# Routed-expert block: every item's rows added into one copy of the output, in a chain, where two alternating copies took them

## The chip, the cores and the metric

The kernel runs on one core of one Trainium2 chip. The metric is the device time of one execution in microseconds (us). The kernel before was timed three times: 1404.11, 1408.82 and 1414.78 us, median 1408.82 us. One more execution was taken with the hardware profiler.

## The reference, cut to what matters

One layer of an encoder: a mixing stage (spatial gating and a Fourier part), then a mixture of 64 experts over 1024 tokens of 1024 channels, all in float32. Only the end of the mixture and the final norm bear on the change:

```
eidx, gates = route(hn, w_router, router_bias)          # 8 of 64 experts per token
routed = routed_experts(hn, eidx, gates, w_gate, w_up, w_down)
    # per block of up to 128 tokens of one expert:
    #   out = (silu(xb @ w_gate[e]) * (xb @ w_up[e])) @ w_down[e] * gate
    #   y = y.at[tok].add(out)
shared = (silu(hn @ ws_gate) * (hn @ ws_up)) @ ws_down
h = h + routed + shared
return rms_norm(h, final_norm_g)
```

## The kernel before

**Stages.** Up to about 450 us the kernel does the mixing stage, the router and the shared expert. Then comes the loop over *items*. An item is one block of up to 128 tokens that chose the same expert; in these inputs there are 93 items for 64 experts, so some experts have one item and some have two or more. Three items are one turn (`TURN = 3`), and buffers that rotate by item have three places, `u = 0, 1, 2`. After the loop comes the final norm over eight blocks of 128 rows.

**One item, engine by engine.** GpSimd (POOL) gathers the item's token rows from `hn_rows_dram` into `Xg` with an indirect DMA, four items ahead. TensorE (PE) transposes them (L464), multiplies by gate and up weights (`gate_up`, L721), transposes the result (`turn_h`, L743) and multiplies by the down weights (`down`, L735). VectorE (DVE) forms `hh` from the silu, the gate value and the up product (`gated_h`, L1290). ScalarE (ACT) copies the result out of PSUM into `ob[:, u, :]` (`evac_out`, L940). POOL then issues an indirect DMA with `compute_op=add` (`add_rows`, L1492; called *the add* below) that adds the 128 rows of `ob`, 512 KB, into rows of `y_rows_dram`. The weights of an expert (3 MB: `raw_gu` twice, `raw_dn` once) are loaded by the sync engine's queue (SP), and ACT and DVE split them into a high and a rest part.

**POOL's order.** In item `i` POOL does, in this order: `keep_gate(i+1)` (waits for the transposes of item i+1, then a small copy of the gate column, L1474), `gather(i+4)` (L1461, L1464), `add_rows(i-1)` (L1481, L1492). POOL works in order, so whatever the add waits for also holds up the next item's gate copy and gather. The gate copied by `keep_gate(i+1)` is first read by DVE's `hh` of item i+1, about one item later.

**Copies of the output.** `y_rows_dram` holds three copies of the output rows, each of `ROWS = 1152` rows. Copy 0 starts as h plus the shared expert; copies 1 and 2 are filled with zeros (L340). Items of even number add into copy 0, those of odd number into copy 1, the last three into copy 2 (`copy_row`, `late_row`). The same row may be named by two items, and an accumulating transfer reads and later writes its row, so two adds into one copy must not be in flight together. With two alternating copies, add `i` waits for the landing of add `i-2`; in the last turn, whose three adds share copy 2, adds wait for the one right ahead.

**The end.** When the adds of all but the last turn have landed and the last weights are split, SP loads copy 0 into `ya_in` (eight transfers of 512 KB, L439) and half of copy 1 into `yb_in` (L441); after the last `gate_up` it loads the other half (L446). DVE adds the two (`both_copies`, L1358, eight instructions). After the last add has landed, SP loads copy 2 into `yc_in` (L452), DVE adds that (`last_copy`, L1363), ACT squares and sums (L789), POOL makes the root (L1412, L1414), DVE scales (L1374) and SP stores (L455).

Of the kernel before, what the change touches and what calls it, by code (L numbers as in the profile page):

```python
# [23 lines left out]
P = 128  # L24
# [38 lines left out]
def build(nc, x, g1, w_in, ln_g, ln_b, wsT, bsT, ga, gb, w_out, g2, w_router, rbias, wg, wu, wd,  # L63
          sg, su, sd, dft_pos, dft_ch, gf, out, hn_d, y_d):
    ctx = ExitStack()
    with ctx:
        top = [nc.sbuf_base]

        def place(name, shape, dt, at=None):

            size = 2 if dt in (BF16, F16) else 4
            n = size
            for s in shape[1:]:
                n *= s
            n = (n + 31) // 32 * 32
            if at is None:
                at = top[0]
                top[0] += n
            return nc.alloc_sbuf_tensor_at(name, shape, dt, offset=at)
# [126 lines left out]
        ya_in = place("ya_in", [P, NC, D], F32, U_AT)  # L206
        yb_in = [place("yb_in0", [P, NC // 2, D], F32, Z_AT), place("yb_in1", [P, NC // 2, D], F32, T_AT)]
        yc_in = place("yc_in", [P, NC, D], F32, X_AT)
# [55 lines left out]
        s_yl = [sem(f"y_last_in{c}") for c in range(NC)]  # L264
        s_both, s_sum = sem("copies_summed"), sem("last_copy_summed")
        s_sqf, s_rf, s_of, s_ost = sem("sqf"), sem("rstdf"), sem("out_rows"), sem("out_stored")
# [6 lines left out]
        yv2 = y_d[ROWS:2 * ROWS, :].rearrange("(c p) d -> c p d", p=P)  # L273
        yv3 = y_d[2 * ROWS:3 * ROWS, :].rearrange("(c p) d -> c p d", p=P)
        y23_flat = y_d[ROWS:3 * ROWS, :].rearrange("(p r) (a f) -> p (r a) f", p=P, f=P)
        dump_flat = y_d[S:ROWS, :].rearrange("p (a f) -> p a f", f=P)
# [38 lines left out]
        def _(sp):  # L315
# [23 lines left out]
            sp.dma_start(dump_flat, zero[:, None, :].to_broadcast([P, KD, P])).then_inc(s_dz, 16)  # L339
            sp.dma_start(y23_flat, zero[:, None, :].to_broadcast([P, 2 * (ROWS // P) * KD, P])).then_inc(s_zst, 16)  # L340

# [96 lines left out]
            for c in range(NC):  # L438
                sp.dma_start(ya_in[:, c, :], yv[c]).then_inc(s_x[c], 16)  # L439
                if c < NC // 2:  # L440
                    sp.dma_start(yb_in[0][:, c, :], yv2[c]).then_inc(s_x[c], 16)  # L441
            last = last_item(sp)
            sp.wait_ge(s_gu, last + 1)
            sp.sem_inc(s_turn_sp, 1)
            for c in range(NC // 2, NC):
                sp.dma_start(yb_in[1][:, c - NC // 2, :], yv2[c]).then_inc(s_x[c], 16)  # L446
            n = turns(sp)
# [3 lines left out]
            for c in range(NC):  # L451
                sp.dma_start(yc_in[:, c, :], yv3[c]).then_inc(s_yl[c], 16)  # L452
            for c in range(NC):
# [548 lines left out]
        def _(dv):  # L1002
# [270 lines left out]
            for c in range(2, NC):  # L1273
                slot_marks(c)
                if c == 5:
                    shared_h(2)
            step(dv.tensor_scalar(late_row[:, :], count_row[:, :], late[:, 0:1], 2.0 * ROWS, ALU.is_ge, ALU.mult))
            step(dv.tensor_tensor(copy_row[:, :], copy_row[:, :], late_row[:, :], ALU.max))
# [76 lines left out]

            def both_copies(c):
                dv.wait_ge(s_x[c], 64)
                dv.tensor_tensor(ya_in[:, c, :], ya_in[:, c, :], yb_in[c // 4][:, c % 4, :], ALU.add).then_inc(s_both, 1)  # L1358

            def last_copy(c):  # L1360
                dv.wait_ge(s_both, c + 1)
                dv.wait_ge(s_yl[c], 16)
                dv.tensor_tensor(ya_in[:, c, :], ya_in[:, c, :], yc_in[:, c, :], ALU.add).then_inc(s_sum, 1)  # L1363

            for c in range(NC):
                both_copies(c)
            last_copy(0)
# [11 lines left out]
        def _(gp):  # L1379
# [60 lines left out]
            for c in range(NC):  # L1440
# [5 lines left out]
                    allow_small_or_imprecise_dtypes=True).then_inc(s_info, 1)  # L1446
            gp.iota(copy_row[:, :], pattern=[[0, TAB // 2], [ROWS, 2]], base=0, channel_multiplier=0,
                    allow_small_or_imprecise_dtypes=True).then_inc(s_info, 1)
# [7 lines left out]
            top_row = gp.to_reg(S - 1)  # L1456
            top_dump = gp.to_reg(3 * ROWS - 1)

# [18 lines left out]
            def add_rows(i, u, turn, same_copy=False):  # L1477

                after(gp, s_add[u], 16 * turn)
                gp.sem_inc(s_turn, 1)  # L1480
                gp.tensor_copy(idxs[:, u:u + 1], row_all[:, bass.ds(i, 1)]).then_inc(s_sc_col, 1)  # L1481
                gp.wait_ge(s_sc_col, i + 1)
                gp.sem_inc(s_turn, 1)
                gp.wait_ge(s_oa, i + 1)
                if same_copy and u > 0:
                    gp.wait_ge(s_add[u - 1], 16 * turn + 16)
                elif u < 2:
                    after(gp, s_add[u + 1], 16 * turn)
                else:
                    gp.wait_ge(s_add[0], 16 * turn + 16)  # L1490
                gp.sem_inc(s_turn, 1)
                gp.indirect_dma_start(out=y_d[:, :], out_offset=bass.IndirectOffsetOnAxis(ap=idxs[:, u:u + 1], axis=0),  # L1492
                                      in_=ob[:, u, :], in_offset=None, compute_op=ALU.add,
                                      bounds_check=top_dump).then_inc(s_add[u], 16)
# [90 lines left out]
```

## Time and profile before

| | |
|---|---|
| median of three runs | 1408.82 us (1404.11 to 1414.78) |
| the profiled execution, device time | 1411.65 us |
| its span, first to last instruction | 1410.0 us |
| TensorE matmuls busy | 1309.5 us, 93% of the span |
| DVE / ACT / POOL busy | 875.7 / 738.1 / 459.0 us |
| DMA moved | 348.47 MB, mean 247 GB/s |
| adds (L1492) | 93, issued from 470.9 to 1368.2 us |
| zero fill of copies 1 and 2 (L340) | 9216 KB, issued at 56.7 us, lands 37.6 us later |
| mean granted TensorE clock | 0.97 of full speed |

How to read it: the span and the device time of the profiled execution differ by 1.65 us, which lie around the instructions. Busy time on an engine says how long its instructions ran; a wait costs time only where it reaches the chain that ends last. POOL's busy time does not hold its waits for semaphores. "Landing" is the time from the issue of a transfer to its completion semaphore.

### The profile page before, as it was taken

What the parts mean: (1) busy time and instruction counts of PE and PEld (TensorE: products, weight loads), DVE (VectorE), ACT (ScalarE), POOL (GpSimd) and SP (SyncE); (2) the same over time, 40 slices, a digit from 0 to 9 for tenths busy, and PEclk for the clock granted to TensorE, in tenths of its full rate; (3) what the DMA queues carried; (4) which work ended last, traced back from release to release, by engine and by line L of the source; (5) the groups of instructions that cost most, each with busy time, mean ns of one, the idle gap of its engine ahead of it and who ended that gap; (6) DMA issues with size and microseconds to landing.
All of it is one profiled execution on the core that took longest, in us unless ns stands there. A gap on an engine that the chain in (4) does not pass through costs nothing.

```text
span 1410.0 us, 25859 instructions
## 1 busy us (share of the span) xinstructions
PE 1309.5 (93%) x5960; PEld 1024.4 (73%) x5962; DVE 875.7 (62%) x1318; ACT 738.1 (52%) x1044; POOL 459.0 (33%) x608
## 2 busy tenths in 40 slices
PE   6899988999999999999989999999999999999960
PEld 5785466888444887888878888788877788888850
DVE  4430444345665676767866567776687666775846
ACT  4421244211011676767865657766677666775822
POOL 1431201000001344434443344334343434443435
PEclk9999999999999999999999999999999999999985
DMA  9464032002306799999999889999899989999987
GB/s 336 150 180 160 0 119 90 40 36 80 152 5 241 248 302 340 327 305 326 339 365 280 259 250 318 363 344 282 253 366 376 325 249 306 325 339 278 295 257 279
DMA packets 99535, 348.47 MB, mean 247 GB/s; under 512 B 13104, under 2 KB 33584, under 8 KB 82736
## 3 DMA queue, kind: packets, MB, share of 16 engines
q1 hardware_dynamic: 72144, 263.64, 48.7%
q0 software_dynamic: 27360, 84.44, 26.4%
q8 instruction: 16, 0.26, 0.1%
q14 instruction: 15, 0.12, 0.0%
HBM read 294.85 MB, written 71.57 MB: 260 GB/s over the span
## 4 chain that ended last, share of the span: by engine, by line
PE 71%; DMA 14%; ACT 3%; issue 3%; DVE 2%; POOL 1%; DVEq 1%; ACTq 1%; SPq 0%; POOLq 0%
PE ps L721 26%; PE ps_out L735 13%; DMA raw_gu<-in_w_up 8%; PE ps L613 6%; PE ps L481 5%; PE ps L464 5%; DMA raw_dn<-in_w_down 5%; PE ps L648 4%; PE ps L515 4%; PE ps L564 2%; ACT w_gu L919 1%; DMA y_rows_dram<-ob,idxs 1%; PE ps_out L630 1%; PE ps L743 1%; PE ps L658 1%
## 5 line engine op out<-in xcount | busy, mean ns | idle before, releaser
L721 PE MATMUL ps<-w_gu,xTh 128*128 x1504 | 477.9, 399 | 13.2 <-DVE xTl L1297 11.1
L1144 DVE TENSOR_TENSOR w_gu<-raw_gu,w_gu (+1 forms) x256 | 302.6, 1223 | 63.8 <-ACT w_gu L919 62.9
L721 PEld LDWEIGHTS ps<-w_gu,xTh 128*128 128x128 f32 x1504 | 279.0, 190 | 73.5 <-issue 19.3
L721 PE MATMUL ps<-w_gu,xTl 128*128 x752 | 296.6, 394 | 0.0
L919 ACT ACTIVATE w_gu<-raw_gu (+1 forms) x256 | 256.8, 1060 | 23.7 <-SPq L387 23.7
L735 PE MATMUL ps_out<-w_dn,hTh 128*128 x744 | 242.1, 407 | 0.0
L1492 POOL DMA_INDIRECT y_rows_dram<-ob,idxs x93 | 151.7, 1632 | 194.8 <-ACT ob L940 175.9
L1151 DVE TENSOR_TENSOR w_dn<-raw_dn,w_dn (+1 forms) x128 | 150.9, 1221 | 84.0 <-ACT w_dn L923 83.6
L721 PEld LDWEIGHTS ps<-w_gu,xTl 128*128 128x128 f32 x752 | 142.6, 190 | 30.0
L735 PEld LDWEIGHTS ps_out<-w_dn,hTh 128*128 128x128 f32 x744 | 133.1, 189 | 25.1
L735 PE MATMUL ps_out<-w_dn,hTl 128*128 x372 | 145.9, 392 | 0.0
L923 ACT ACTIVATE w_dn<-raw_dn (+1 forms) x128 | 128.4, 1057 | 31.8 <-SPq L391 31.6
L1297 DVE TENSOR_TENSOR xTl<-ps,xTh 128x512 fp32r<-128x512 f32 x188 | 120.9, 685 | 26.0 <-ACT xTh L934 26.0
L1464 POOL DMA_INDIRECT Xg<-hn_rows_dram,idxg x97 | 105.7, 1089 | 79.0 <-POOL idxg L1461 76.9
L1474 POOL COPY gate<-Xg 128x1 f32 x94 | 37.4, 398 | 287.6 <-PE ps L464 166.0
L934 ACT ACTIVATE xTh<-ps 128x512 fp32r<-128x512 f32 x188 | 102.3, 597 | 51.5 <-PE ps L464 51.5
L929 ACT ACTIVATE hs<-ps 128x256 f32<-128x256 f32 x93 | 35.7, 384 | 151.4 <-PE ps L721 151.0
L464 PEld LDWEIGHTS ps<-ident,Xg 128*128 128x128 f32 x752 | 98.0, 190 | 8.1 <-issue 0.5
L1412 POOL TENSOR_SCALAR rs<-ms 128x1 f32<-128x1 f32 x40 | 25.8, 645 | 239.9 <-ACT junk L789 238.3
L940 ACT ACTIVATE ob<-ps_out 128x1024 f32<-128x1024 f32 x93 | 95.1, 1022 | 7.0 <-PE ps_out L735 7.0
L464 PE MATMUL ps<-ident,Xg 128*128 128x128 f32 x752 | 98.3, 274 | 0.0
L1290 DVE SCALAR_TENSOR_TENSOR hh<-hs,gate,ps 128x256 f32<-128x256 f32 x93 | 44.6, 479 | 63.3 <-ACT hs L929 44.0
(206 smaller groups left out, 1554.8 us busy)
## 6 DMA issues: line engine op xcount, KB each, us to landing
raw_gu<-in_w_gate SPq DMA_DIRECT2D x64, 1024.0 KB, 7.5
raw_gu<-in_w_up SPq DMA_DIRECT2D x64, 1024.0 KB, 10.8
raw_dn<-in_w_down SPq DMA_DIRECT2D x64, 1024.0 KB, 14.8
y_rows_dram<-zero SPq DMA_DIRECT2D x1, 9216.0 KB, 37.6
x_ring<-in_x SPq DMA_DIRECT2D x8, 512.0 KB, 5.0
w_in_sb<-in_w_in SPq DMA_DIRECT2D x8, 512.0 KB, 9.7
xh<-in_x SPq DMA_DIRECT2D x8, 512.0 KB, 8.2
w_out_sb<-in_w_out SPq DMA_DIRECT2D x1, 4096.0 KB, 12.9
```

What stands on the lines that cost most here:

```text
L464: last = pe.transpose(ps[banks[k // 4]][:, (k % 4) * P:(k % 4 + 1) * P], src[:, k:D:KD], ident[:, :])
L721: mm = pe.matmul(ps[3][:, :], x_[:, k, :], w_gu[:, bass.ds(at, 1), part, :, k, :], start=(k == 0 and part == 0 and x_ is xTh), stop=(k == ...
L735: mm = pe.matmul(ps[6 + half][:, :], h_[:, k, :], w_dn[:, bass.ds(at, 1), part, k, half * 512:(half + 1) * 512], start=(k == 0 and part == ...
L919: act.activation(gu_part(w_gu[:, :, 0, :, :, :], at, m), gu_part(raw_gu, at, m), ACT.Copy).then_inc(s_hg, 1)
L923: act.activation(w_dn[:, bass.ds(at, 1), 0, k, :], raw_dn[:, bass.ds(at, 1), k, :], ACT.Copy).then_inc(s_hd, 1)
L934: act.activation(xTh[:, half * 4:half * 4 + 4, :], ps[1 + half][:, :].rearrange("p (k t) -> p k t", k=4), ACT.Copy).then_inc(s_xa, 1)
L940: act.activation(ob[:, u, :], ps_out[:, :], ACT.Copy).then_inc(s_oa, 1)
L1144: dv.tensor_tensor(gu_part(w_gu[:, :, 1, :, :, :], at, m), gu_part(raw_gu, at, m), gu_part(w_gu[:, :, 0, :, :, :], at, m).bitcast(F32), AL ...
L1151: dv.tensor_tensor(w_dn[:, bass.ds(at, 1), 1, k, :], raw_dn[:, bass.ds(at, 1), k, :], w_dn[:, bass.ds(at, 1), 0, k, :].bitcast(F32), ALU.s ...
L1297: dv.tensor_tensor(xTl[:, part, :], ps[1 + half][:, :].rearrange("p (k t) -> p k t", k=4), xTh[:, part, :].bitcast(F32), ALU.subtract).the ...
L1464: gp.indirect_dma_start(out=Xg[:, u, :], out_offset=None, in_=hn_d[:, :], in_offset=bass.IndirectOffsetOnAxis(ap=idxg[:, u:u + 1], axis=0) ...
L1492: gp.indirect_dma_start(out=y_d[:, :], out_offset=bass.IndirectOffsetOnAxis(ap=idxs[:, u:u + 1], axis=0), in_=ob[:, u, :], in_offset=None, ...
```

## The change

Items of even and odd number now add into the same copy, copy 0; the last three add into the second copy, which takes the place of the third. The memory tensor shrinks from three copies to two, the zero fill from 9 MB to 4.5 MB. Every add waits for the landing of the add right ahead of it, across turns too. At the end only one copy is loaded before the last adds have landed, `yb_in`, its eight loads and the eight DVE additions of `both_copies` are gone, and `last_copy` waits for the load of copy 0 itself.

```diff
-            sp.dma_start(y23_flat, zero[...].to_broadcast([P, 2 * (ROWS // P) * KD, P])).then_inc(s_zst, 16)
+            sp.dma_start(y2_flat, zero[...].to_broadcast([P, (ROWS // P) * KD, P])).then_inc(s_zst, 16)
...
             for c in range(NC):
                 sp.dma_start(ya_in[:, c, :], yv[c]).then_inc(s_x[c], 16)
-                if c < NC // 2:
-                    sp.dma_start(yb_in[0][:, c, :], yv2[c]).then_inc(s_x[c], 16)
-            last = last_item(sp)
-            sp.wait_ge(s_gu, last + 1)
-            sp.sem_inc(s_turn_sp, 1)
-            for c in range(NC // 2, NC):
-                sp.dma_start(yb_in[1][:, c - NC // 2, :], yv2[c]).then_inc(s_x[c], 16)
             n = turns(sp)
...
-                sp.dma_start(yc_in[:, c, :], yv3[c]).then_inc(s_yl[c], 16)
+                sp.dma_start(yc_in[:, c, :], yv2[c]).then_inc(s_yl[c], 16)
...
-            step(dv.tensor_scalar(late_row[:, :], count_row[:, :], late[:, 0:1], 2.0 * ROWS, ALU.is_ge, ALU.mult))
+            step(dv.tensor_scalar(late_row[:, :], count_row[:, :], late[:, 0:1], float(ROWS), ALU.is_ge, ALU.mult))
...
-            def both_copies(c):
-                dv.wait_ge(s_x[c], 64)
-                dv.tensor_tensor(ya_in[:, c, :], ya_in[:, c, :], yb_in[c // 4][:, c % 4, :], ALU.add).then_inc(s_both, 1)
             def last_copy(c):
-                dv.wait_ge(s_both, c + 1)
+                dv.wait_ge(s_x[c], 48)
                 dv.wait_ge(s_yl[c], 16)
...
-            gp.iota(copy_row[:, :], pattern=[[0, TAB // 2], [ROWS, 2]], base=0, channel_multiplier=0,
+            gp.iota(copy_row[:, :], pattern=[[0, TAB]], base=0, channel_multiplier=0,
...
                 gp.wait_ge(s_oa, i + 1)
-                if same_copy and u > 0:
+                if u > 0:
                     gp.wait_ge(s_add[u - 1], 16 * turn + 16)
-                elif u < 2:
-                    after(gp, s_add[u + 1], 16 * turn)
                 else:
-                    gp.wait_ge(s_add[0], 16 * turn + 16)
+                    after(gp, s_add[TURN - 1], 16 * turn)
                 gp.sem_inc(s_turn, 1)
```

## Rows read from the trace of the kernel before

**Rows 1.** Windows: PE, PEld, DVE, ACT, POOL busy, PEclk, DMA share, GB/s.

```profile
565.00:690.00 125.00, 124.87 (x609) 103.51 (x608) 91.57 (x108) 89.67 (x123) 52.91 (x67) 1.00 0.98 317
...
750.00:860.00 110.00, 110.00 (x540) 91.76 (x539) 66.65 (x82) 65.99 (x94) 43.93 (x58) 1.00 0.89 262
...
1040.00:1120.00 80.00, 72.54 (x333) 58.56 (x332) 61.29 (x70) 59.79 (x79) 31.15 (x36) 0.96 1.02 369
```

**Rows 2.** The line of the adds, L1492, over the whole run, with landing times.

```profile
L1492 POOL DMA_INDIRECT y_rows_dram<-ob,idxs x93: 1585/1605/2247, 470.9 to 1368.2; - x93
...
  POOL y_rows_dram L1492: 8.9, 1
...
DMA to landing us min/median/max: 6.0/9.2/11.1
```

**Rows 3.** Timeline of one item on POOL: start, duration, instruction, idle before it.

```profile
809.76 1.60 POOL L1492 DMA_INDIRECT y_rows_dram<-ob,idxs  x1 [2.34 <-ACT ob L940]
814.16 0.18 POOL L1474 COPY gate<-Xg 128x1 f32 x1 [2.79 <-DVE hh L1290]
...
815.47 1.06 POOL L1464 DMA_INDIRECT Xg<-hn_rows_dram,idxg  x1 [0.80 <-POOL idxg L1461]
```

**Rows 4.** Timeline of the same stretch on DVE.

```profile
822.81 0.48 DVE L1290 SCALAR_TENSOR_TENSOR hh<-hs,gate,ps 128x256 f32<-128x256 f32 x1 [0.83 <-ACT hs L929]
```

**Rows 5.** Waits by engine: waiter, releaser, us in total, times, longest.

```profile
DVE hh L1290 <- POOL gate L1474: 18.2, 14, 4.2
```

**Rows 6.** The line of the adds from 565 to 690 us.

```profile
L1492 POOL DMA_INDIRECT y_rows_dram<-ob,idxs x13: 1605/1605/1607, 568.0 to 681.4; - x13
...
DMA to landing us min/median/max: 6.0/9.9/10.5
```

**Rows 7.** The same from 750 to 860 us.

```profile
L1492 POOL DMA_INDIRECT y_rows_dram<-ob,idxs x12: 1605/1606/2247, 753.5 to 856.6; - x12
...
DMA to landing us min/median/max: 6.0/6.8/9.4
```

**Rows 8.** The same from 1040 to 1120 us.

```profile
L1492 POOL DMA_INDIRECT y_rows_dram<-ob,idxs x8: 1605/1605/1906, 1044.7 to 1118.9; - x8
...
DMA to landing us min/median/max: 6.5/9.6/10.1
```

**Rows 9.** The add issued at 518.0 us alone, then that at 605.8 us.

```profile
L1492 POOL DMA_INDIRECT y_rows_dram<-ob,idxs x1: 1605/1605/1605, 518.0 to 518.0; - x1
...
DMA to landing us min/median/max: 10.9/10.9/10.9
...
L1492 POOL DMA_INDIRECT y_rows_dram<-ob,idxs x1: 1605/1605/1605, 605.8 to 605.8; - x1
...
DMA to landing us min/median/max: 9.9/9.9/9.9
```

**Rows 10.** The chain that ended last, its pieces at the end: start, us, what.

```profile
1356.94 10.44 DMA y_rows_dram<-ob,idxs
...
1368.22 9.08 DMA y_rows_dram<-ob,idxs
1377.39 4.00 DMA yc_in<-y_rows_dram
```

**Rows 11.** Timeline of the end, ACT and DVE.

```profile
1363.08 1.02 ACT L940 ACTIVATE ob<-ps_out 128x1024 f32<-128x1024 f32 x1 [7.05 <-PE ps_out L735]
...
1378.42 2.48 DVE L1358 TENSOR_TENSOR ya_in<-ya_in,yb_in 128x1024 f32<-128x1024 f32 x2 [0.33 <-DMA yb_in<-y_rows_dram]
...
1381.48 1.23 DVE L1363 TENSOR_TENSOR ya_in<-ya_in,yc_in 128x1024 f32<-128x1024 f32 x1 [0.58 <-DMA yc_in<-y_rows_dram]
```

**Rows 12.** SP's late loads of copy 1, line L446.

```profile
L446 SPq DMA_DIRECT2D yb_in<-y_rows_dram x4: 320/432/2449, 1358.2 to 1359.5; - x4
...
DMA to landing us min/median/max: 15.2/18.8/20.1
```

**Rows 13.** Timeline of SP after the zero fill.

```profile
117.39 5.08 SPq L344 DMA_DIRECT2D xh<-in_x  x8
```

More of the change, by code:

```diff
@@ L206, in build @@
         ya_in = place("ya_in", [P, NC, D], F32, U_AT)
-        yb_in = [place("yb_in0", [P, NC // 2, D], F32, Z_AT), place("yb_in1", [P, NC // 2, D], F32, T_AT)]
         yc_in = place("yc_in", [P, NC, D], F32, X_AT)
@@ L264, in build @@
         s_yl = [sem(f"y_last_in{c}") for c in range(NC)]
-        s_both, s_sum = sem("copies_summed"), sem("last_copy_summed")
+        s_sum = sem("copies_summed")
         s_sqf, s_rf, s_of, s_ost = sem("sqf"), sem("rstdf"), sem("out_rows"), sem("out_stored")
@@ L273, in build @@
         yv2 = y_d[ROWS:2 * ROWS, :].rearrange("(c p) d -> c p d", p=P)
-        yv3 = y_d[2 * ROWS:3 * ROWS, :].rearrange("(c p) d -> c p d", p=P)
-        y23_flat = y_d[ROWS:3 * ROWS, :].rearrange("(p r) (a f) -> p (r a) f", p=P, f=P)
+        y2_flat = y_d[ROWS:2 * ROWS, :].rearrange("(p r) (a f) -> p (r a) f", p=P, f=P)
         dump_flat = y_d[S:ROWS, :].rearrange("p (a f) -> p a f", f=P)
@@ L339, in _ @@
             sp.dma_start(dump_flat, zero[:, None, :].to_broadcast([P, KD, P])).then_inc(s_dz, 16)
-            sp.dma_start(y23_flat, zero[:, None, :].to_broadcast([P, 2 * (ROWS // P) * KD, P])).then_inc(s_zst, 16)
+            sp.dma_start(y2_flat, zero[:, None, :].to_broadcast([P, (ROWS // P) * KD, P])).then_inc(s_zst, 16)
             sp.wait_ge(s_za, 2 * NC)
@@ L1353, in _ @@
                 turn_of_items(t)
-            def both_copies(c):
-                dv.wait_ge(s_x[c], 64)
-                dv.tensor_tensor(ya_in[:, c, :], ya_in[:, c, :], yb_in[c // 4][:, c % 4, :], ALU.add).then_inc(s_both, 1)
             def last_copy(c):
-                dv.wait_ge(s_both, c + 1)
+                dv.wait_ge(s_x[c], 48)
                 dv.wait_ge(s_yl[c], 16)
                 dv.tensor_tensor(ya_in[:, c, :], ya_in[:, c, :], yc_in[:, c, :], ALU.add).then_inc(s_sum, 1)
-            for c in range(NC):
-                both_copies(c)
             last_copy(0)
@@ L1456, in _ @@
             top_row = gp.to_reg(S - 1)
-            top_dump = gp.to_reg(3 * ROWS - 1)
+            top_dump = gp.to_reg(2 * ROWS - 1)
             def gather(i, u):
@@ L1577 @@
     hn_d = nc.dram_tensor("hn_rows_dram", (S, GATED), F32, kind="Internal").ap()
-    y_d = nc.dram_tensor("y_rows_dram", (3 * ROWS, D), F32, kind="Internal").ap()
+    y_d = nc.dram_tensor("y_rows_dram", (2 * ROWS, D), F32, kind="Internal").ap()
     build(nc, h["x"], h["norm1_g"], h["w_in"], h["sgu_ln_g"], h["sgu_ln_b"], h["w_spatial"], h["b_spatial"],
```

## The prediction

> **What bounds the kernel now.** I read the busy time by stretches first. In the loop TensorE is all but never idle where experts have several items (124.87 of 125 us, 110.00 of 110 us), while the DMA engines are nearly full too (0.98, 0.89); where every item brings a new expert the DMA engines are the bound (1.02) and TensorE waits a little (72.54 of 80 us) [rows 1]. So the loop is set by TensorE, in places by the weight loads. POOL, on which the change puts its wait, is busy for 52.91 us of the first and 43.93 us of the second stretch.
>
> Then the line of the adds. 93 adds were issued between 470.9 and 1368.2 us, one each 897.3/92 = 9.75 us; they took 6.0 to 11.1 us to land, in the median 9.2, and only once in the run, for 8.9 us, did one wait for another [rows 2]. So the pace of the adds was set by the items, and a landing is about as long as an item. That is the whole question: a chain in which each add waits for the one ahead has for its period the landing plus the price of the hand-over.
>
> **The hand-over.** The one add that waited gives it: the add ahead was issued at 1356.94 and landed 10.44 us later, at 1367.38; the waiting one started at 1368.22 [rows 10]. That is 0.84 us.
>
> **The chain against the items.** I read the landing of each of the 93 adds by a window of its own (two of them are shown [rows 9]). Their sum is 791.4 us, the mean 8.51 us. Chain: 8.51 + 0.84 = 9.35 us; items: 9.75 us. On the average the chain keeps up by 0.4 us per add, but not everywhere. From 565 to 690 us the 13 landings have a mean of 8.89 (median 9.9 [rows 6]), the chain needs 9.73 and the items come every 9.45: lateness grows by 0.28 us per add, 3.7 over the stretch. From 750 to 860 us the mean is 7.34 (median 6.8 [rows 7]), the chain needs 8.18 against 9.38 and gains 1.2 us per add. In the dense stretch from 1040 to 1120 us it needs 9.23 + 0.84 = 10.07 and adds come every 74.2/7 = 10.6 us [rows 8].
>
> I carry the lateness from add to add: late(next) = max(0, start + late + landing + 0.84 - start of the next). The worst run begins with the add at 518.0, which lands in 10.9 us and has its successor 9.35 us later: 10.9 + 0.84 - 9.35 = 2.4 us late. Ten adds on, after that at 605.8 [rows 9], the lateness peaks at 6.2 us. It is above zero for 67 of 93 adds and 0.0 for the last two.
>
> **What is behind the waiting add, and how late it may be.** On POOL there are the next gate copy and the next gather. Example: add at 809.76, 1.60 us long, ends at 811.36; the gate copy comes at 814.16 anyway, so 2.8 us are idle [rows 3]. The gate copied at 814.16 is that of the item whose `hh` runs at 822.81 [rows 4]; copy plus hand-over take 0.4 us. So an add may be late by 822.81 - 0.4 - 811.36 = 11.0 us before DVE, and then TensorE, waits. The waits put 18.2 us on `hh` waiting for the gate copy [rows 5], which would deny this slack; by the code the copy that lies just before an `hh` belongs to the following item, so I read these 14 as wrongly attributed. The gather serves an item four on, some 28 us later after a landing of under 10 us. `ob` has three places and is overwritten about 26 us after the add's issue: 26 - 11 = 15 us. The gate is the tightest, at 11.0 us, and the peak of 6.2 is inside it. **The loop: 0 us.** This is the choice on which all depends. Bounds: below, 0 (no engine gets less work in the loop); above, if late adds all landed as the loaded ones do (9.9 to 10.5, medians and tops of rows 6) the chain would need 10.7 to 11.3 us in every stretch that now goes at 9.4 and the loss would be tens of us (rival 1).
>
> **Does lateness lengthen the landings?** A landing is near 6 us when the add falls between two weight loads and 9 to 11 us when it is beside one (33 of 93 are below 7.3 us). A late add that was issued just ahead of a load moves into it, and one that was in a load moves to its end; the DMA work is the same. Past 2.8 us of lateness the next gather is issued right behind the add instead of at its end. If the gather stands behind the add, the add isn't slowed; if the two share, it is. What speaks for the first is the dense stretch: adds come late there because their `ob` is late (one every 10.6 us), the next gather follows sooner than elsewhere, and still no landing is over 10.1 us [rows 8], less than the 10.5 and 10.9 where the order is the usual one [rows 6, 9]. I take the first, and allow for 5 to 9 us of lateness instead of 6.2, which the 11.0 still cover; the margin is thin.
> The Trainium skill ("DMA: Bandwidth & Descriptors", section "Two DMAs through the same engine are not ordered") says that within one queue descriptors start in order, though completions aren't ordered. By that rule the gather goes behind the add and the loop costs 0; by sharing it costs what rival 1 says. No row here shows either alone.
>
> **The end of the kernel.** Before: the last but one add is issued at 1356.94 and lands in 10.44 us, the last in 9.08, at 1377.30; `yc_in` is then asked for and its first block lands 4.00 us later; `last_copy(0)` starts at 1381.48 [rows 10, 11]. All this time SP's queue is full: the four late loads of copy 1 are issued by 1359.5 and land in up to 20.1 us, at about 1379.5 [rows 12]. The change takes 8 x 512 KB off that queue, half of what it moves before `yc_in`. The queue then is empty at about 1366 (half of the 28 us from the first load of `ya_in` at 1351.4 to 1379.5, plus the share of the add). So
> - the last but one add still lies mostly beside the loads of copy 0: 10.44 to about 9.8, gain 0.6 (bounds 0 and 10.4 - 6.2 = 4.2, of which only 3.2 count, since `ob` of the last item is written at 1364.10 [rows 11] and its add can't start before about 1365);
> - the last add lies alone: 9.08 to about 6.3, the landing of adds beside no load (minimum 6.0 [rows 2]), gain 2.8 (bounds 0 and 3.1);
> - the first block of `yc_in` has no rest of copy 1 ahead of it: 4.00 to about 3.5, gain 0.5 (bounds 0 and 0.7).
>
> Sum 3.9 us, bounds 0 and 7.0. The eight additions L1358 (1.24 us each) win nothing by themselves: their last ends at 1380.90, before `yc_in` lands at 1381.39 [rows 10, 11]; had they stayed, they'd now be the bound, but they go with the loads. From `last_copy(0)` on the instructions are the same.
>
> **The rest.** The zero fill of 9216 KB, which lands at 94.3, becomes half of it; the next transfer on SP's queue is at 117.39 [rows 13], and the wait for the fill is at 470 us: 0 us. Changed constants, one iota pattern, and as many waits as before: 0 us.
>
> **The sum.** 1410.0 - 3.9 = 1406.1 us of span. The profiled execution (1411.65) is 2.8 us above the median of the three runs; the same 3.9 off the median 1408.8 is 1404.9, **1405 us**.
>
> **Rivals.**
> 1. *The chain of adds becomes the bound of the loop.* Once late, each add has the whole next gather in its landing, and lands in 10.5 us (the top of rows 6) wherever weights are loaded: 10.5 + 0.84 = 11.3 against 9.4 us per item. Over the 27 adds of 565 to 690 and 1190 to 1320 us that is 27 x 1.9 = 51 us, less the 11.0 us that the gate allows: +40; light and dense stretches can't give this back once TensorE has waited. With the gain of the end: 1408.8 + 40 - 4 = 1445 us. Half of it (the landings of half of these adds rise) is 27 x 0.95 - 11 - 4 = +11, 1420 us. It decides from a mean landing of about 8.9 us on (9.75 - 0.84), only 0.4 above the present mean: this speaks for it; against it stands that DMA work isn't added and that light stretches give 1.2 us per add. Chance 0.28, of which 0.25 are over 1% slower.
> 2. *The end gives nothing*, because the last adds are slow by themselves and not by the loads beside them: 1409 us. Against it: the adds between loads land in 6.0 to 6.5 us. Chance 0.12.
> 3. *The end gives its upper bound and the loop a little more*, adds no longer ever lying beside another add: 1408.8 - 7 and some 3 for loads that come earlier, 1399 us; for more than 1% faster TensorE's 110.00 of 110 us leaves no room. Chance 0.10, of which 0.04 are over 1% faster.
>
> **How the numbers follow.** The forecast (loop 0, end 3 to 6 us) has 0.50: 1400 to 1409 with the scatter of a median of three. About 1% is what a measurement of this kernel can tell from no change: below 1394.7 faster, above 1422.9 slower. Faster 0.04, within 0.71, slower 0.25. The range for 8 in 10 runs from 1399 (rival 3) to 1430, which leaves out the full rival 1.
>
> **What would show it.** In the profile after: POOL waits of `y_rows_dram` for `y_rows_dram` in some 60 places with a total near 100 us; POOL's gate copy up to 4 us later than now, and yet `hh` released by ACT's `hs`; TensorE at 110 of 110 us in a stretch with two items per expert. Wrong: `hh` waiting for the gate in long waits of several us, TensorE idle in the 565 to 690 us stretch, and adds one behind another at 10.5 us plus 0.84. For the end: the last add landing about 6.3 us after its issue, and from there to `last_copy(0)` under 4 us.

## The result: slower by 1.6%, and where the time went

The changed kernel takes 1432.88 us (median of four runs, 1430.35 to 1435.55) against 1410.31 us of the kernel before; the ratio is 1.0158, with a 95% interval of 1.0137 to 1.0178. The forecast was 1405 us with a range up to 1430: wrong in sign and just outside the range. Rival 1, the chain as the bound of the loop, is what came: the loop costs 22.1 us, where its full size was 40.

In the profiled executions the span goes from 1410.0 to 1433.9 us, +23.9. First the line of the adds in the profile after, with its landing times (count and first and last start; who waited; landing):

```profile
L1475 POOL DMA_INDIRECT y_rows_dram<-ob,idxs x93: 1583/1690/2671, 470.1 to 1395.8; - x93
...
  DMA y_rows_dram<-ob,idxs: 428.5, 86
...
DMA to landing us min/median/max: 6.1/9.8/11.9
```

(The middle line is the idle time that ended with the landing of another add: us, times.) Against [rows 2]: the add waited for another one 86 times instead of once, 428.5 us in all instead of 8.9, and the median landing rose from 9.2 to 9.8. The adds now come every (1395.8 - 470.1)/92 = 10.06 us instead of 9.75. The chain that ended last runs through DMA transfers, nearly all of them landings of the adds, for more than half of the span, where before it ran through TensorE (PE 71%, DMA 14%):

```profile
DMA 58%; PE 29%; issue 5%; POOL 1%; POOLq 1%; ACT 1%; DVE 1%; DVEq 0%; ACTq 0%; SPq 0%
```

The windows after (PE, PEld, DVE, ACT, POOL busy, clock, DMA share, GB/s) answer to [rows 1]:

```profile
565.00:690.00 125.00, 124.86 (x608) 103.57 (x607) 91.70 (x109) 89.74 (x123) 56.15 (x62) 1.00 0.95 310
...
750.00:860.00 110.00, 106.34 (x517) 87.48 (x516) 62.21 (x78) 64.81 (x93) 42.08 (x55) 1.00 0.85 256
```

The loss is not where I had looked for it. From 565 to 690 us TensorE is as full as before, as lateness only builds up there. From 750 to 860 us, the light stretch that was to give the lateness back, TensorE loses 3.7 of 110 us (in the dense stretch from 1040 to 1120 us 2.1 of 80), and the DMA share *falls* from 0.89 to 0.85: nothing is overloaded, TensorE and the queues wait in turn for a chain of single transfers.

How a wait for an add gets to TensorE is seen in one place. POOL's timeline after:

```profile
745.16 2.19 POOL L1475 DMA_INDIRECT y_rows_dram<-ob,idxs  x1 [2.99 <-DMA y_rows_dram<-ob,idxs]
...
757.40 1.61 POOL L1475 DMA_INDIRECT y_rows_dram<-ob,idxs  x1 [7.46 <-DMA y_rows_dram<-ob,idxs]
758.48 0.73 POOL L1459 COPY gate<-Xg 128x1 f32 x1
```

and VectorE's:

```profile
759.30 0.48 DVE L1281 SCALAR_TENSOR_TENSOR hh<-hs,gate,ps 128x256 f32<-128x256 f32 x1 [3.44 <-POOL gate L1459]
```

The rows of `ob` for the add at 757.40 were ready at 741.64 (an ACT copy of 1.02 us begun at 740.62): it is 15.8 us late, and its predecessor, issued at 745.16, landed only after 11.4 us. Right behind it comes the gate copy, and `hh` has waited 3.44 us for that. In the whole run there are 38 such waits of `hh`, 88.4 us; before the page had 14 with 18.2 us [rows 5], which I had read as wrongly attributed.

**The sum of the +23.9 us.** The last `ob` is written at 1386.16 instead of 1364.10 [rows 11]: the loop costs 22.1 us. From there to `last_copy(0)` it is 19.6 us instead of 17.4, +2.2: the last add is issued 9.6 us after its rows are ready instead of 4.1 (+5.5), but from its issue to `last_copy(0)` it takes 10.0 us instead of 13.3 (-3.2). The rest to the end is 0.4 us shorter. 22.1 + 2.2 - 0.4 = 23.9. The last rows of the chain after, against [rows 10]:

```profile
1388.37 6.55 DMA y_rows_dram<-ob,idxs
...
1395.76 6.30 DMA y_rows_dram<-ob,idxs
1402.15 3.54 DMA yc_in<-y_rows_dram
```

### The profile page after: what moved, and what is told of

It reads as the page before. It is cut to its first block, busy times and chain, and to the rows that moved or that the text cites. A ratio compares the mean times of both kernels' runs of the same rounds, so it can differ in the third digit from the quotient of the medians.

```text
span 1433.9 us, 25867 instructions
## 1 busy us (share of the span) xinstructions
PE 1314.4 (92%) x5960; PEld 1022.7 (71%) x5962; DVE 865.2 (60%) x1310; ACT 737.2 (51%) x1044; POOL 461.3 (32%) x608
## 3 DMA queue, kind: packets, MB, share of 16 engines
q0 software_dynamic: 27360, 84.44, 25.7%
## 4 chain that ended last, share of the span: by engine, by line
DMA 58%; PE 29%; issue 5%; POOL 1%; POOLq 1%; ACT 1%; DVE 1%; DVEq 0%; ACTq 0%; SPq 0%
DMA y_rows_dram<-ob,idxs 58%; PE ps L604 6%; PE ps L472 5%; PE ps L639 4%; PE ps L506 4%; PE ps L555 2%; PE ps L712 2%; PE ps_out L621 1%; PE ps L649 1%; PE ps_out L649 1%; PE ps L455 1%; PE ps L567 1%; POOLq L303 1%; PE ps_out L726 1%; POOL rs L1397 1%
## 5 line engine op out<-in xcount | busy, mean ns | idle before, releaser
L1475 POOL DMA_INDIRECT y_rows_dram<-ob,idxs x93 | 174.2, 1873 | 459.1 <-DMA y_rows_dram<-ob,idxs 428.5
L910 ACT ACTIVATE w_gu<-raw_gu (+1 forms) x256 | 256.9, 1059 | 28.1 <-SPq L385 28.1
L1449 POOL DMA_INDIRECT Xg<-hn_rows_dram,idxg x97 | 108.8, 1121 | 79.1 <-POOL idxg L1446 77.0
L1281 DVE SCALAR_TENSOR_TENSOR hh<-hs,gate,ps 128x256 f32<-128x256 f32 x93 | 44.6, 480 | 132.2 <-POOL gate L1459 88.4
L1459 POOL COPY gate<-Xg 128x1 f32 x94 | 78.5, 835 | 48.2 <-PE ps L455 41.4
## 6 DMA issues: line engine op xcount, KB each, us to landing
w_in_sb<-in_w_in SPq DMA_DIRECT2D x8, 512.0 KB, 10.2
```

Of the source, the lines that this page charges most:

```text
L910: act.activation(gu_part(w_gu[:, :, 0, :, :, :], at, m), gu_part(raw_gu, at, m), ACT.Copy).then_inc(s_hg, 1)
L1449: gp.indirect_dma_start(out=Xg[:, u, :], out_offset=None, in_=hn_d[:, :], in_offset=bass.IndirectOffsetOnAxis(ap=idxg[:, u:u + 1], axis=0) ...
```

## The experiments

Two terms were used throughout. *Lateness* is the time from the end of ACT's copy into `ob` to the add's start, read from the timelines of ACT and POOL for all 93 adds; it is 0.95 us in the mean in the kernel before, and 11.99 (at most 17.6) in the changed one. It counts from the rows' being ready, so a usual add has 0.95 already. *Hand-over* is the time from a landing to the next add's start; over the 58 places of the changed kernel where both are known it is 0.82 us (0.77 to 0.88). Where a trace had no landing of an add, I took the distance to the next waiting add less 0.81.

### The two halves of the change, each alone

*Only the chain.* The kernel before with this in `add_rows`:

```diff
-                if same_copy and u > 0:
-                    gp.wait_ge(s_add[u - 1], 16 * turn + 16)
-                elif u < 2:
-                    after(gp, s_add[u + 1], 16 * turn)
-                else:
-                    gp.wait_ge(s_add[0], 16 * turn + 16)
+                if u > 0:
+                    gp.wait_ge(s_add[u - 1], 16 * turn + 16)
+                else:
+                    after(gp, s_add[TURN - 1], 16 * turn)
```

> The kernel before with its three copies, its loads and its additions at the end, and only the wait of the adds changed: each waits for the add right ahead. Theory W (the wait is the cost: the chain of landing plus 0.84 us has become the pace of the loop): the adds come every 10.0 to 10.1 us as in the changed kernel, POOL waits for the adds over 400 us in total, and the time is that of the changed kernel plus what the shorter end gave it: 1434 to 1440 us. Rival M (the memory: adds into one copy take longer than adds into alternating copies, in the same rows' neighbourhood): the landing falls back to a mean of 8.5 us and the time to 1405 to 1415 us.

Measured: 1438.52 us against 1410.01, ratio 1.0202 (1.0182 to 1.0222), +28.5 us. The line of the adds:

```profile
L1490 POOL DMA_INDIRECT y_rows_dram<-ob,idxs x93: 1585/1614/2641, 471.1 to 1395.3; - x93
...
  DMA y_rows_dram<-ob,idxs: 416.7, 84
...
DMA to landing us min/median/max: 6.1/9.7/11.9
```

Alternating copies, and yet the same pace (10.05 us), the same waits and landings. That the adds go into one place in memory is no part of the cost; rival M falls.

*Only the end.* The kernel before without the loads of copy 1 and without `both_copies`:

```diff
-                if c < NC // 2:
-                    sp.dma_start(yb_in[0][:, c, :], yv2[c]).then_inc(s_x[c], 16)
...
-            for c in range(NC // 2, NC):
-                sp.dma_start(yb_in[1][:, c - NC // 2, :], yv2[c]).then_inc(s_x[c], 16)
...
-                dv.wait_ge(s_both, c + 1)
+                dv.wait_ge(s_x[c], 48)
```

> The kernel before with its alternating copies and waits, but copy 1 is neither loaded nor added at the end, so the rows of the items of odd number are missing from the output. The prediction's step on the end: from the last add's issue to last_copy(0) 13.3 us before, about 9.9 here, the time 3 to 5 us under the kernel before (1405 to 1407). Rival: the last adds are slow by themselves, the end is as long as before, 1409 to 1411.

Measured: 1405.28 against 1410.01 us, ratio 0.9954 (0.9931 to 0.9976), -4.7 us. By the time the 3.9 us of the prediction hold. By the steps 3.1 us are seen: from the last add's issue to `last_copy(0)` it is 10.2 us instead of 13.3 (the expectation said 9.9). The rest of the profiled pair is not the end's doing: the last `ob` is written 3.1 us later, and the part after `last_copy(0)` takes 24.9 us instead of 28.5, a difference of some 3 us that comes and goes between runs whose code is the same there (28.1 in the changed kernel, 25.7 in the run with only the chain). The sum of the halves is 28.5 - 4.7 = +23.8, the whole change 22.6.

### What makes the landing long: the gather or the weight loads

*Gathers that move nothing*, in the changed kernel and in the kernel before:

```diff
+            no_row = gp.to_reg(0)
...
-                gather(i + 1 + TURN, (u + 1) % TURN)
+                gather(i + 1 + TURN, (u + 1) % TURN, no_row)     # bounds_check=no_row
```

> The changed kernel, but from the fifth item on the gathers find nearly all their indices out of bounds and move nothing (old rows are computed on instead), so about 0.5 MB less per item goes through the queue that the adds share. Theory G (late adds land late because the next gather lies in their landing): the mean landing falls from 9.35 by 1 us or more, the chain needs under 9.3 us, and the loop is bound by the items again: below 1412 us, possibly below the kernel before. Rival L (the weight loads beside the add set its landing): the landing falls by under 0.4 us, and the time stays over 1423 us.

> The same taken away from the kernel before, as the measure for the run above. By both theories TensorE sets the loop, so the time falls only where the weight loads set it: 1395 to 1410 us. The landings of the adds without a gather beside them: theory G about 7.5 us in the mean, rival L about 8.2.

Measured: with the chain 1393.98 us, ratio 0.9884 (0.9852 to 0.9916); without it 1389.92, 0.9855 (0.9829 to 0.9881). The chain and the shorter end together now cost 4 us instead of 23; with the 4.7 us of the end taken off, the chain alone costs about 9 instead of 28. The adds of the chain still wait, but the gate copy behind them is waited for far less (waits of the chain without gathers: us, times, longest):

```profile
POOL y_rows_dram L1477 <- DMA y_rows_dram<-ob,idxs: 319.2, 77, 7.5
...
DVE hh L1281 <- POOL gate L1461: 24.4, 9, 5.1
```

Their mean landing is 8.69 us (82 adds) instead of 9.19 (90 adds of the changed kernel): 0.5 us, half of what theory G said, more than rival L allowed. The trace of the control has no landings, so that its expectation on them can't be judged. But 8.69 + 0.82 = 9.51 is just the pace of the items there, (1351.6 - 469.9)/92 = 9.58 against 9.53 in the control: the mean lateness stays at 8.8 us, on the near side of the gate's 11. As the adds are also less late there (8.8 us against 12.0), the half us is the effect of the missing gathers and of the smaller lateness together.

*Half of each weight load*, in the changed kernel:

```diff
+              w_[e].rearrange("(p k) f -> p k f", k=KD)[:, 0:KD // 2, :]).then_inc(s_gu_in[at], 16)
...
+          wd[e].rearrange("(k p) d -> p k d", p=P)[:, 0:1, :]).then_inc(s_dn_in[at], 16)
```

> The changed kernel, but from the third expert on only half of each weight (half of the k blocks of gate and up, one of two of down) is loaded, the other half is old data; 1.5 instead of 3 MB per expert lie beside the adds, and the gathers are whole. Theory L (what lengthens a late add's landing is above all the weight load it lies beside): the mean landing falls from 9.2 to 8.0 us or less, lateness stays under 8 us, the adds come every 9.4 us as the items do, and the time is 1370 to 1395 us. Rival G (above all the gather behind it): landing 8.7 us or more, lateness over 8 us for most adds, 1405 us or more.

Measured: 1383.9 us against 1413.19, ratio 0.9797 (0.9767 to 0.9827). The line of the adds:

```profile
L1484 POOL DMA_INDIRECT y_rows_dram<-ob,idxs x93: 1583/1607/2200, 467.5 to 1343.4; - x93
...
  DMA y_rows_dram<-ob,idxs: 10.2, 2
...
DMA to landing us min/median/max: 5.9/6.5/10.1
```

The same chain, gathers whole, and the adds wait twice instead of 86 times. The mean landing is 6.91 us, and 60 of the 93 are below 7.3 us. The adds are on time there (0.96 us late in the mean), so the run says nothing about late adds; its fair partner is the kernel before, whose adds are on time too: 8.51 us with the whole loads beside them, 6.91 with half. What makes a landing long is first the weight load beside it (theory L); either one, taking the gathers away or halving the loads, is enough to bring the chain back to the pace of the items. The Trainium skill ("DMA: Bandwidth & Descriptors", section "Queues, rings and completion order") says that each DMA engine goes round between the queues it has work for, a packet of each at a time; that fits a landing which depends on what SP's queue holds, though no run here shows the turns themselves. The adds themselves are no more work than before: the packets of the software queue, which holds adds and gathers, took 26.4% of 1410.0 = 372 us before and 25.7% of 1433.9 = 369 us after.

*Where the late adds fall.* This needs no further run: the traces of both kernels have the time of each add and of each weight load. One add of the light stretch before, issued at 837.90, and one after, issued at 802.88; for each its landing and the next weight load on SP's queue:

```profile
DMA to landing us min/median/max: 6.1/6.1/6.1
...
840.99 0.33 SPq L281 DMA_DIRECT2D raw_gu<-in_w_gate  x1
```

```profile
DMA to landing us min/median/max: 11.9/11.9/11.9
...
804.28 0.33 SPq L279 DMA_DIRECT2D raw_gu<-in_w_gate  x1
```

The first is issued 3.1 us before the next load and lands in 6.1 us, the second 1.4 us before it and lands in 11.9. The whole run has the same picture. Before, no add is issued less than 2.5 us ahead of a load, and 60 are issued 2.5 to 4 us ahead; 30 of these land in less than 7.3 us. After, 30 adds are issued less than 2.5 us ahead of a load, and none of them lands in less than 8.0 us; their mean is 9.9 (the run with only the chain has 30 such adds too, with a mean of 9.9). Counted over all adds, landings below 7.3 us fall from 33 of 93 to 19 of 90. The short ones have a mean of 6.3 us before and 6.5 after, the long ones 9.7 and 9.9. So of the 0.68 us by which the mean landing grew, some 0.5 come from short landings that turned long, and 0.2 from longer landings of either kind. One thing weakens this a little: in 25 of the 30 POOL's own add instruction also takes more than 1.8 us, where 1.6 is usual.

### How lateness becomes time: the mean, or the work behind the wait

*A dearer hand-over.* In the changed kernel the copy of the row numbers is done after the wait instead of before it:

```diff
-                gp.tensor_copy(idxs[:, u:u + 1], row_all[:, bass.ds(i, 1)]).then_inc(s_sc_col, 1)
-                gp.wait_ge(s_sc_col, i + 1)
...
                     after(gp, s_add[TURN - 1], 16 * turn)
                 gp.sem_inc(s_turn, 1)
+                gp.tensor_copy(idxs[:, u:u + 1], row_all[:, bass.ds(i, 1)]).then_inc(s_sc_col, 1)
+                gp.wait_ge(s_sc_col, i + 1)
```

> The changed kernel with a dearer hand-over: POOL's copy of the row numbers, some 1 us with its wait, is done after the wait for the add ahead instead of before it. Theory R (rate: the mean of landing plus hand-over is the pace of the loop, 10.06 us per item): every us put into the hand-over is paid at nearly every add, so 88 adds x 1.0 = +88 us, about 1520 us, at the least 1490. Rival S (slack: the loop loses only where a single late add passes the 11 us that the gate copy allows, and gets the rest back): under half of that, below 1475 us.

Measured: 1488.38 us against 1410.68, ratio 1.0561 (1.0517 to 1.0605), 55.5 us over the changed kernel. That is between the two expectations (1490 and 1475) and settles nothing between them. The adds come every 10.68 us instead of 10.06, and their landings are shorter, 9.01 us in the mean of all 93. The rest of the pace is the hand-over: 1.67 us, where the same sum gives 0.87 in the changed kernel. So 0.8 us were put in, not the 1.0 of the expectation, and 0.62 of them came through at each add; the slower pace gave 0.18 back in the landings.

*The gate copy on VectorE*, behind `rest_xT`, with POOL's gather waiting for it; in both kernels:

```diff
-                gp.tensor_copy(gate[:, u:u + 1], Xg[:, u, bass.ds(e + D, 1)]).then_inc(s_gt, 1)
...
+                keep_gate(i + 1, (u + 1) % TURN)      # in VectorE's item: dv.tensor_copy(gate...)
```

> The changed kernel with the copy of the gate column made by VectorE, so that hh no longer waits for POOL, which stands at the add. Theory R (rate): the chain of adds still needs 10.06 us per item, and only some 4 us more of lateness are allowed, by ob, once in the run: 1425 to 1433 us. Rival S (slack, the gate copy behind the waiting add is the cost): hh no longer waits, the loop goes at the items' pace, 1403 to 1412 us.

> The same move in the kernel before, as the measure for the run above: the gate copy isn't waited for there, VectorE gets some 0.3 us more per item beside TensorE. Both theories: within 6 us of the kernel before, 1405 to 1416 us.

Measured: with the chain 1415.94 us, 1.0039 (1.0019 to 1.0058); in the kernel before 1415.02, 1.0037 (1.0019 to 1.0055). The move costs 4 to 5 us by itself, and the change costs 1 us more with it instead of 23. What the chain still costs is then about what the end gives, 5 to 6 us. I had expected the opposite, 1425 to 1433 us by the theory I then held.

*The gate copy one item earlier on POOL*, in both kernels:

```diff
-                keep_gate(i + 1, (u + 1) % TURN)
+                keep_gate(i + 2, (u + 2) % TURN, turn + 1 if u + 2 < TURN else turn + 2)   # waits for s_ga[u], not s_tr
+                gp.wait_ge(s_tr, i + 2)
...
                 gather(i + 1 + TURN, (u + 1) % TURN)
```

> The changed kernel with POOL's gate copy made one item earlier (as soon as the rows of the item after next have landed), so that an add may be late by one item more (some 20 us instead of 11) before hh waits; nothing goes to VectorE. Theory S (the gate copy queued behind the waiting add turns lateness into TensorE stalls): hh waits for the gate no longer, and the time falls from 1433 to 1408 to 1414 us, some 4 us less than with the copy on VectorE. Rival R (the chain's mean period of 10.06 us is a property of the adds): lateness grows by 0.3 us per add, uses up the further 9 us, and the time is 1424 us or more.

> The same move in the kernel before: the gate isn't waited for there, so both theories give no change, 1407 to 1413 us; the landings keep their mean of 8.5 us.

Measured: with the chain 1417.2 us, ratio 1.0039 (1.0013 to 1.0064); in the kernel before 1411.67, ratio 1.0010 (0.9994 to 1.0026). So the chain as it is, every add still waiting for the one ahead, costs 16 us less when only the gate copy is taken out from behind the wait. The time is 3 us above what theory S allowed (1408 to 1414 us) and 7 below rival R's; against its own control the change still costs 5.5 us, which with the 4.7 of the end makes some 10 for the chain. Its waits:

```profile
POOL y_rows_dram L1475 <- DMA y_rows_dram<-ob,idxs: 380.9, 84, 7.5
...
DVE hh L1281 <- POOL gate L1459: 3.6, 1, 3.6
```

and its windows:

```profile
750.00:860.00 110.00, 110.00 (x543) 91.76 (x542) 68.54 (x85) 67.29 (x97) 44.24 (x58) 1.00 0.88 260
```

The adds wait as before, 84 times, and are later than ever (15.1 us in the mean, at most 21.7), but TensorE is full again, 110.00 of 110 us, and the last `ob` is written at 1364.64, within 0.6 us of the kernel before (1.2 of the control with the same move). The loop's loss is gone but for that. What stays of +5.5 us in the spans is the end: the last add is issued 12.5 us after its rows (4.1 before), 8.4 us later, less 3.0 us from its issue to `last_copy(0)`. The next limit is in sight too: ACT waits ten times, 14.2 us in all, for an add to leave `ob`.

*Each add in two halves*, each chained to the same half of the one ahead:

```diff
+                for h in range(2):
+                    gp.wait_ge(s_add[u - 1][h], 16 * turn + 16)       # u = 0: the last of the turn before
+                    gp.indirect_dma_start(out=y_half[:, :], ..., in_=ob[:, u, h * 512:(h + 1) * 512], ...)
```

> The changed kernel with each add cut into two transfers of half the columns, each half waiting only for the same half of the add ahead: one copy of the output as before, but two chains, so that one half's hand-over and descriptor making lie beside the other half's data. Theory R (rate): the price of 0.8 us and of POOL's instruction (1.9 us) leaves the chain; its period falls from 10.06 to under 9.5 us, the loop is bound by the items, and with the shorter end the time is 1402 to 1410 us. Rival D (the DMA engines' work itself sets the landing): two halves take as long as the whole and POOL makes two instructions of 1.6 us, 1430 us or more.

Measured: 1438.54 us against 1410.68, ratio 1.0212 (1.018 to 1.0244). The forecast of the theory I tested it for fails, and rival D's number comes (it had said 1430 us or more); the software queue has 40752 packets instead of 27360 and `hh` waits 91.3 us for the gate, as in the changed kernel. The trace has no landings of the halves, so it can't be said whether the data or POOL's second instruction (186 of 1.59 us in the median) ate the gain, and it shows neither theory right.

### Lateness without a chain

*Adds late on purpose.* The kernel before, with the add issued behind the next transposes' wait and ahead of the gate copy:

```diff
-                keep_gate(i + 1, (u + 1) % TURN)
+                gp.wait_ge(s_tr, i + 2)
...
+                    add_rows(i - 2, (u - 2) % TURN, turn if u == 2 else turn - 1, same_copy and u == 2)
+                keep_gate(i + 1, (u + 1) % TURN, True)
                 gather(i + 1 + TURN, (u + 1) % TURN)
...
-                    add_rows(i - 1, (u - 1) % TURN, turn if u else turn - 1, same_copy and u > 0)
```

> The kernel before with its two alternating copies and without a chain, but each add is issued late on purpose: one place later in POOL's program, right after the transposes of the item after, so some 4.4 us after its usual time and with the next gather right behind it. It measures what lateness alone does to the landing. Theory G (late adds land later, having the gather beside them): mean landing 9.0 us or more instead of 8.5. The prediction's assumption: still 8.5 us. Time by both: 1408 to 1413 us, as nothing waits for the adds.

Measured: 1417.65 us, ratio 1.0053 (1.0035 to 1.0071), above the 1408 to 1413 that both expected. The adds are 6.7 us late in the mean. In the profiled execution the last `ob` is written 5.6 us later than before, for a reason I have not found, and the last add is issued 11.0 us after its rows instead of 4.1; the part behind it is shorter. The trace holds no landing of an add, so this run does not answer the question it was made for.

## Why the prediction was wrong, point by point

- **What bounds the kernel before, the hand-over, the pace.** Right: TensorE, 0.84 us from one place against 0.82 in 58, 9.75 us per item.
- **The chain against the items: the step that failed.** The prediction took each add's landing (mean 8.51 us) as a property of the add and moved only the starts. In the changed kernel it is 9.19 us, and the chain needs 10.0 us instead of 9.35, more than the items' 9.75. It failed most where all the safety lay, in the light stretch. From [rows 7] I had 7.34 us and a recovery of 1.2 us per add. After, the line of the adds from 750 to 860 us reads

```profile
L1475 POOL DMA_INDIRECT y_rows_dram<-ob,idxs x11: 1607/1869/2624, 757.4 to 854.9; - x11
...
DMA to landing us min/median/max: 6.1/9.2/11.9
```

  that is a pace of (854.9 - 757.4)/10 = 9.75 us; nine of these ten gaps are waits for the add ahead, and the mean landing of the ten is 8.8. With the hand-over the chain needs 9.7 us here, where the items came every 9.38. Before, every other add of this stretch was issued some 3 us ahead of the next weight load and 15.7 us behind the last one, whose slowest part lands in 14.8 us in the median; most of these adds landed in about 6.1 us. That moment belonged to the add's *place in time*, not to the add. A late add misses it and shares with a load: the 30 adds issued less than 2.5 us ahead of one land in 9.9 us in the mean, none in less than 8.0. The prediction saw this possibility ("a late add that was issued just ahead of a load moves into it") and argued it away by an exchange: others would move out of loads. They didn't in equal number: landings below 7.3 us fell from 33 of 93 to 19 of 90, and in the light stretch three of eleven still land in 6.1 or 6.2 us, where six of twelve took 6.0 to 6.5.
- **"The gather behind the add doesn't slow it."** It is not shown that a gather slows the add by sharing. With gathers the mean landing is 9.19, without them 8.69, but the adds are less late without them, too. It may be the gather behind this add, the one still moving when the next add starts, or the smaller lateness; no run tells these apart. Where no load is beside it, a gather issued 3.0 us behind the add does not show: the add at 757.40 lands in 6.1 us all the same. What is shown is that without the gathers 4 us are lost, not 23: the margin is so thin that half a us in the landing decides.
- **The 11.0 us until the gate copy is late.** Right as the place, and near enough as the size: with the copy an item earlier or on another engine the loop's loss is gone. In the changed kernel 52 of 93 adds are over it (more than 11.9 us from `ob` to issue). I had called the peak 6.2, with an allowance to 9; it is 16.6 over the usual 0.95.
- **The waits of `hh` for the gate** [rows 5]. Setting the 14 old ones aside cost nothing, by the control: with the copy an item earlier they vanish from the kernel before (one is left, of 4.2 us), and its time does not change (1.0010, 0.9994 to 1.0026). In the changed kernel such waits are real, since taking them out was worth 16 us.
- **The end.** -3.9 us predicted, -4.7 measured alone; the landing of the last add 6.3 predicted, 6.30 measured; `yc_in` 3.5 and 3.54; from issue to `last_copy(0)` 3.2 us won of 3.3. The 0.6 us for the last add but one did not come in the way described: with only the end changed it lands in about 10.3 us (the gap to the last add, 11.09, less the hand-over), where 9.8 was forecast for 10.44. But the end isn't free of the loop: the chain hands over a late last add, and 5.5 us of that are lost ahead of the gain.
- **Zero fill, constants.** Nothing of the sum of +23.9 is left for them.
- **Rival 1** had the right bound (the chain sets the pace) and the threshold (mean landing of 8.9; it is 9.19). Its reason for it, the whole next gather in each late landing, is at most a part: most of the growth is short landings that turned long. Of its three numbers the chance was furthest off, 0.28 being small for a margin of 0.4 us in 9.75. Its lower size was 1420, its upper 1445; 1433 lies between. Its working put the loss into the mixed stretches, where 51 us were to arise, from 565 to 690 us among them. By the shift of ACT's copies into `ob` against the same items before, nothing is lost up to 700 us (-2.6 us); after that the loss grows through light and mixed stretches alike: +3.4 us at 855, +12.6 at 1136, +21.9 at 1325.

What stays open: how much of the longer landings is the gather, and why POOL's own add instruction grew from 1632 to 1873 ns in the mean. As the landing is counted from its start, its growth of 0.24 us may be a part of the 0.68; that was not tested. It does not lie beside VectorE's work more often than before, by the timelines. No version that was tried beats the kernel before; the one with only the end changed is faster because it leaves work out.

## What to carry to other kernels

A landing time read from a trace belongs to the moment at which the transfer was issued as much as to the transfer: when a change moves the moment, take the landing that such transfers have in the company of the loads (here 9 to 11 us, up to 11.9), not the mean of the old schedule, and distrust any margin that rests on the short ones. Before putting a long wait on an in-order queue, list what stands behind it and move out what others need soon: here one small copy, made an item earlier, was worth 16 of the 28 us that the wait cost. And two buffers for an accumulating target were cheap here (4.7 us at the end) against a chain of single transfers (28.5 us).

## What the runs showed of the hardware that I had not expected

- The landing of one and the same indirect add of 512 KB ranges from 5.9 to 11.9 us, above all with what the other queue carries: mean 6.91 us with half of the weight loads and 8.51 with all of them, the adds on time in both; 9.19 in the chain. In the pair shown above an add issued 3.1 us ahead of a weight load landed in 6.1 us, one issued 1.4 us ahead of it in 11.9.
- A serial chain of transfers lowers the DMA engines' share (0.89 to 0.85 from 750 to 860 us) while it is the bound.
- The gate copy of 128 x 1 on POOL went from a mean of 398 ns to 835 ns between the two pages, with nothing changed in it. Two things go with its length. Alone, with VectorE idle, it takes 0.18 us (49 copies before, all 0.18 or 0.19); beside an instruction of VectorE 0.64 in the mean (41 copies before). And begun while POOL's own add instruction still runs, as at 758.48 above, it takes 0.73 us even with VectorE idle (32 copies after, 0.72 to 0.74), and 1.28 with VectorE busy (23). After the change 85 of the 91 copies are begun so, before only one.
